# The fourth weight sum of the down projection: VectorE additions, or accumulating transfers within SBUF

## The chip, the cores and the metric

One NeuronCore of a Trainium2 chip. The metric is the device time of one execution in microseconds (us). The engines are named as the profile names them: PE (TensorE, matmul), DVE (VectorE), ACT (ScalarE), POOL (GpSimd) and SP (SyncE, which here only starts transfers). Transfers started by SP go through one queue, those started by POOL through another, and both are served by the same 16 DMA engines. A transfer that adds to its destination instead of overwriting it is started by POOL in this kernel.

## What is computed

One decoder layer on 512 positions of 2048 features: a mixer (a gated short convolution beside an mLSTM), a normalisation, a gated feed-forward part with a short convolution, and a second normalisation. The change lies in the last matrix product of the feed-forward part, the down projection.

```
hid = x @ w_up                         # 512 x 2048 times 2048 x 11264
hid = causal_dwconv(hid, w_ffn_conv, b_ffn_conv)
val, gate = hid[:, :5632], hid[:, 5632:]
ff  = (silu(gate) * val) @ w_down      # 512 x 5632 times 5632 x 2048
out = layer_norm(alpha * x + ff)
```

All inputs are float32. The kernel gets float32 accuracy from reduced-precision products: each operand is split into a high part and a low part (the operand less its high part), and three products of parts are added up (`mm3`).

## The kernel before

The down projection works by Strassen's scheme in Winograd's form: instead of eight block products there are seven, named P1, P2, P6, P5, P7, P3 and P4 in the order in which they run (`ORDER`, with index i from 0 to 6). Their operands are blocks of the weights and of the hidden activations, or sums of blocks. The weights have four blocks, A11, A12, A21 and A22, each 128 partitions by 1024 columns for every pair of contraction tiles. They are held in SBUF in the buffers `da11`, `da12`, `da21`, `da22`, and a fifth buffer `dx` takes a sum.

The contraction is cut into six chunks of 4, 4, 4, 4, 3 and 3 pairs (`CHUNK_PAIRS`; c is the chunk, p the pair). One chunk runs its seven products one after the other, each over all pairs. A slot is one (c, i, p): 12 matmuls. There are 154 slots.

Four weight sums are made for each pair:

- S1: `da21` += A22, an accumulating transfer from HBM, started by POOL, two pairs at a time (`down_s1`, L686);
- S2: `dx` = `da21` + `da11`, an addition on DVE (`down_s2`, L1669), the operand of P6;
- S3: `da11` += A21, an accumulating transfer from HBM (`down_s3`, L694), the operand of P7;
- S4: `da12` += `dx`, an addition on DVE (`down_s4`, L1681, its instruction at L1685), the operand of P3.

S4 may run when S2 of that pair is done and when P2, which uses `da12` as it was, has had its operand of that pair split. The next chunk's S2 overwrites `dx` and therefore waits for S4.

For each slot ACT makes the weights' high part (`down_split`, L1065) and DVE the low part (`down_lo_part`, L1651, recorded at L1655), into one of five slot buffers. Both work four slots ahead of PE (`DOWN_AHEAD`); a buffer comes free when PE has done the slot five before. The hidden activations of a product are split likewise, ACT's part in `hid_split` (L1086, recorded at L1101) and DVE's at L1663 or L1666.

PE's results stand in PSUM. DVE adds them to `acc` in SBUF (`add_out`, L1687, recorded at L1698), two halves a product, in the first two slots of the following product; a few products are the first for their part of `acc` and are copied by ACT (L1127). A product may start when the one two before has been taken out of PSUM.

DVE runs its work in one hand-written order: for each slot s the low part of slot s + 4, then `add_out`, then the weight sums that `sums_after(s)` (L361) names. S4 of pair 0 comes after the last slot of i = 1, of pairs 1 and 2 after that of i = 2, and of pair 3 after that of i = 3. S2 of the next chunk's pairs 0 and 1 comes after i = 5, pair 2 after i = 6.

POOL's order for a chunk (loop at L736): t1 and t2 (subtractions on hidden blocks; not in chunk 0, where DVE does them), S3 in two transfers, t3, t4 (subtractions again, L719 and L725), S1 of the next chunk in two transfers once `da21` has been loaded. In chunks 0 and 1 transfers that add the residual to `acc` (`add_residual`) stand in between. An instruction that waits holds up everything behind it on POOL.

SP's order for the next chunk is `load_hidden` and `load_block` in turn (L534, L529). The first of them waits for t4; the later ones wait until a buffer's operand has been split for the last time. In the up projection, which runs before, the fourth sum of that product is already made by such a transfer within SBUF: `up_s4`, recorded at L667, half a MB each.

Of the kernel before, what the change touches and what calls it, by code (L numbers as in the profile page):

```python
# [7 lines left out]
ALU = mybir.AluOpType  # L8
# [26 lines left out]
CHUNK_PAIRS = [4, 4, 4, 4, 3, 3]  # L35
# [95 lines left out]
def build(nc, x_t, x_rows, w_mix, w_out, w_up, w_down, b_gates, conv_w, gain, ln1_cols, ffn_conv,  # L131
          ln1_rows, ln2_rows, ident_in, head_rows_in, causal_in, out):
    ctx = ExitStack()
    with ctx:
        def at(name, shape, offset, dt=F32):
            return nc.alloc_sbuf_tensor_at(name, shape, dt, offset=offset)

        def sem(name):
            return ctx.enter_context(nc.semaphore(name))
# [75 lines left out]
        da12 = at("da12", [P, 4, 1024], XB + 16 * KB)  # L215
        da21 = at("da21", [P, 4, 1024], XB)
        da22 = at("da22", [P, 4, 1024], XB + 32 * KB)
        dx = at("dx", [P, 4, 1024], XB + 48 * KB)
# [74 lines left out]
        s2_down, s4_down = sem("s2_down"), sem("s4_down")  # L293
        t1_sum, t2_sum, t3_sum, t4_sum = sem("t1_sum"), sem("t2_sum"), sem("t3_sum"), sem("t4_sum")
        hc_lo = sem("hc_lo")
        down_hi, down_lo, down_done, half_done = sem("down_hi"), sem("down_lo"), sem("down_done"), sem("half_done")
# [36 lines left out]
        def unit_of(n):  # L333
            return n // NP + 1, n % NP
# [14 lines left out]
        def slot_no(c, i, p):  # L349
            return SLOT0[c] + i * CHUNK_PAIRS[c] + p  # L350
# [10 lines left out]
        def sums_after(s):  # L361

            c, i, p = DOWN[s]
            g = CHUNK_PAIRS[c]
            todo = []
            if i == 0 and c == 0:
                todo.append(("S2", 0, p))
            elif i == 0 and p == 3:
                todo.append(("S2", c, 3))
            if i in (1, 2, 3) and p == g - 1:  # L370
                todo += [("S4", c, a) for a in {1: [0], 2: [1, 2], 3: [3]}[i] if a < g]
            if i in (5, 6) and p == g - 1 and c + 1 < CHUNKS:
                todo += [("S2", c + 1, a) for a in {5: [0, 1], 6: [2]}[i]]
            return todo

        def out_blocks(c):
# [220 lines left out]
        def _(pool):  # L597
# [96 lines left out]
            def down_s3(c, p):  # L694

                n, w = sum(CHUNK_PAIRS[:c]) + p, min(2, CHUNK_PAIRS[c] - p)
                pool.wait_ge(s2_down, n + w)
                pool.wait_ge(down_lo, slot_no(c, 0, p) + w)
                pool.dma_start(da11[:, p:p + w, :], w_down[A21, :, 1024 * n:1024 * (n + w)].rearrange("p (k n) -> p k n", k=w),
                               accum_op=ALU.add, max_dma_last_dim=4096).then_inc(s3_added[p // 2], 16)  # L700

            def down_t1(c, g):
                for b in range(2):
                    pool.wait_ge(hb_in[b], 16 * (c + 1))
                pool.wait_ge(hc_lo, NP * c)
                pool.tensor_tensor(hy[:, 0:g, :], hb12[:, 0:g, :], hb11[:, 0:g, :], ALU.subtract).then_inc(t1_sum, 1)

            def down_t2(c, g):
                pool.wait_ge(hb_in[3], 16 * (c + 1))
                pool.wait_ge(t1_sum, OUT_CHUNKS + c + 1)  # L710
                pool.wait_ge(hc_lo, NP * c + 1)
                pool.tensor_tensor(hb11[:, 0:g, :], hb22[:, 0:g, :], hy[:, 0:g, :], ALU.subtract).then_inc(t2_sum, 1)

            def down_t3(c, g):
                pool.wait_ge(hb_in[3], 16 * (c + 1))
                pool.wait_ge(t1_sum, OUT_CHUNKS + c + 1)
                if c == 0:
                    pool.wait_ge(down_lo, slot_no(0, 3, 0))
                pool.tensor_tensor(hb12[:, 0:g, :], hb22[:, 0:g, :], hb12[:, 0:g, :], ALU.subtract).then_inc(t3_sum, 1)  # L719
# [16 lines left out]
            for c in range(CHUNKS):  # L736
                g = CHUNK_PAIRS[c]
                if c:
                    down_t1(c, g)
                    down_t2(c, g)  # L740
                for p in range(0, g, 2):
                    down_s3(c, p)
                down_t3(c, g)
                if c == 1:
                    add_residual(0, 1, NP)
                down_t4(c, g)
                if c == 0:
                    add_residual(0, 0, 2)
                if c + 1 < CHUNKS:
                    for p in range(0, CHUNK_PAIRS[c + 1], 2):  # L750
                        down_s1(c + 1, p)
                if c == 0:
                    add_residual(1, 1, 5)
                    add_residual(1, 0, 6)
            pool.wait_ge(out_bias, 16 * BIAS_BY_DMA)
            n = 0
# [8 lines left out]
        def _(act):  # L765
# [276 lines left out]
            for n in range(N_UP):  # L1042
                m, i = unit_of(n)
# [6 lines left out]
                if n in (3, 4):  # L1050
                    t, c = n - 3, 4 * (n - 3)
# [13 lines left out]
            def down_split(s):  # L1065

                c, i, p = DOWN[s]
                what = ORDER[i]
                if s < DOWN_SLOTS:
                    act.wait_ge(up_done, min(N_UP - 2 + s, N_UP))  # L1070
                else:
                    act.wait_ge(down_done, s - DOWN_SLOTS + 1)
                n = sum(CHUNK_PAIRS[:c]) + p
                if what in ("P1", "P2", "P4"):
                    if p == 0:
                        act.wait_ge(da_in[BLOCK[what]], 16 * (c + 1))
                elif what in ("P5", "P7"):
                    if p % 2 == 0:
                        act.wait_ge({"P5": s1_added, "P7": s3_added}[what][p // 2],
                                    16 * (OUT_CHUNKS + sum(CHUNK_PAIRS[a] > p for a in range(c + 1))))  # L1080
                else:
                    act.wait_ge({"P6": s2_down, "P3": s4_down}[what], n + 1)
                src = (da11, da12, da21, da22, dx)[BLOCK[what]]
                act.activation(dslot_hi[s % DOWN_SLOTS][:, :], src[:, p, :], ACT.Copy).then_inc(down_hi, 1)

# [27 lines left out]
            for s in range(N_DOWN):  # L1113
                c, i, p = DOWN[s]
# [30 lines left out]
        def _(dve):  # L1145
# [313 lines left out]
            for s in range(N_OUT):  # L1459
                k, p = s // OUT_PAIRS, s % OUT_PAIRS  # L1460
                c, i = k // NP, k % NP
# [161 lines left out]
            for n in range(N_UP):  # L1623
                m, i = unit_of(n)
# [44 lines left out]
            def down_s2(c, p):  # L1669

                if p == 0:
                    dve.wait_ge(da_in[A11], 16 * (c + 1))
                if p % 2 == 0:
                    dve.wait_ge(s1_added[p // 2], 16 * (OUT_CHUNKS + sum(CHUNK_PAIRS[a] > p for a in range(c + 1))))
                if c:
                    dve.wait_ge(s4_down, sum(CHUNK_PAIRS[:c]))
                else:
                    dve.wait_ge(up_done, N_UP - NP + 4)
                dve.tensor_tensor(dx[:, p, :], da21[:, p, :], da11[:, p, :], ALU.add).then_inc(s2_down, 1)  # L1679

            def down_s4(c, p):  # L1681
                n = sum(CHUNK_PAIRS[:c]) + p
                dve.wait_ge(s2_down, n + 1)
                dve.wait_ge(down_lo, slot_no(c, 1, p) + 1)
                dve.tensor_tensor(da12[:, p, :], da12[:, p, :], dx[:, p, :], ALU.add).then_inc(s4_down, 1)  # L1685

            def add_out(k, u):  # L1687

# [11 lines left out]
            def out_stats(row, fd):  # L1700
                for q in (2 * fd, 2 * fd + 1):
                    dve.bn_stats(bstat[:, row, q, :], acc[:, row, 512 * q:512 * q + 512]).then_inc(ln_step, 1)  # L1702
# [33 lines left out]
            for s in range(N_DOWN):  # L1736
                c, i, p = DOWN[s]
                k = NP * c + i
                if p == 0 and k < last_k:
                    hid_lo_part((k + 1) // NP, (k + 1) % NP)  # L1740
                if s + DOWN_AHEAD < N_DOWN:
                    down_lo_part(s + DOWN_AHEAD)
                if p < 2 and k and k - 1 not in FIRST_TOUCH:
                    add_out(k - 1, p)
                    th, fd = TARGET[ORDER[(k - 1) % NP]]
                    if c == CHUNKS - 1 and ORDER[i - 1] in ("P2", "P7", "P3") and i:
                        dve.wait_ge(added, 2 * (k - 1) + p + 1)
                        out_stats(2 * th + p, fd)
                if s == 0:
                    g = CHUNK_PAIRS[0]  # L1750
                    for b in range(2):
                        dve.wait_ge(hb_in[b], 16)
                    dve.tensor_tensor(hy[:, 0:g, :], hb12[:, 0:g, :], hb11[:, 0:g, :], ALU.subtract).then_inc(t1_sum, 1)
                if s == 1:
                    dve.wait_ge(hb_in[3], 16)
                    dve.wait_ge(t1_sum, OUT_CHUNKS + 1)
                    dve.wait_ge(hc_lo, 1)
                    dve.tensor_tensor(hb11[:, 0:g, :], hb22[:, 0:g, :], hy[:, 0:g, :], ALU.subtract).then_inc(t2_sum, 1)
                for what, chunk, pair in sums_after(s):
                    (down_s2 if what == "S2" else down_s4)(chunk, pair)  # L1760
            out_var(0, 12)
            out_var(1, 12)
            finish(0)
# [437 lines left out]
```

## Time and profile before

| | us |
|---|---|
| median of three runs | 2176.48 |
| lowest and highest run | 2165.42, 2182.86 |
| profiled execution, first to last instruction | 2176.2 |
| of it the down projection's matmuls, first to last start | 1724.94 to 2152.30 |
| mean granted TensorE clock, share of full | 0.994 |

The page gives for each engine its busy time in the span. The timeline lists instructions in order of start; the bracket at the end of a line is the time for which the engine had been idle, and what released it. Matmuls overlap, so their pace is read from the distance of their starts, not from the duration of one. The windows give the busy time of each engine in a stretch, the granted clock, and the mean busy share of the 16 DMA engines, which can come out a little above 1. Times are counted from the first instruction.

### The profile page before, as it was taken

How to read it: one execution, taken by the hardware profiler on the slowest of the kernel's cores; microseconds unless marked ns; L12 is line 12 of the kernel's file. 1: busy time of each engine (PE TensorE's matmuls, PEld its weight loads, DVE VectorE, ACT ScalarE, POOL GpSimd, SP SyncE). 2: the span in 40 equal slices, each digit the busy share in tenths (PEclk: the TensorE clock that was granted, in tenths of full speed). 3: DMA queues.
4: the chain of work that ended last, by engine and by line, in shares of the span. 5: the costliest groups of instructions: out<-in, count | busy, mean ns of one | idle time of the engine just before them, and what ended most of it. 6: DMA issues, size and time to landing. Idle time of an engine off the chain costs nothing. (4 is left out here: it accounts for less than half of the span.)

```text
span 2176.2 us, 26843 instructions
## 1 busy us (share of the span) xinstructions
PE 2125.9 (98%) x10583; PEld 1789.3 (82%) x10583; DVE 1594.2 (73%) x1860; ACT 948.3 (44%) x1107; POOL 267.1 (12%) x241
## 2 busy tenths in 40 slices
PE   9999999999999998999999999999999999999995
PEld 7888888888888887788888888888888788888874
DVE  4354324423338997988888888888888789999998
ACT  3332222221124446555555555555555464444442
POOL 0000000000001304011111111111111023221220
PEclk9999999999999999999999999999999999999998
DMA  6222222242227626888888887887778888775463
GB/s 238 97 97 78 92 89 91 78 171 98 98 79 232 181 73 162 219 241 231 218 207 210 238 219 197 212 229 209 187 203 209 274 228 219 210 237 145 140 193 78
DMA packets 93754, 375.88 MB, mean 173 GB/s; under 512 B 8908, under 2 KB 21228, under 8 KB 80320
## 3 DMA queue, kind: packets, MB, share of 16 engines
q1 hardware_dynamic: 63328, 263.22, 34.4%
q0 software_dynamic: 30304, 110.99, 26.3%
q8 instruction: 82, 1.34, 0.3%
q14 instruction: 40, 0.33, 0.0%
HBM read 326.46 MB, written 26.21 MB: 162 GB/s over the span
## 5 line engine op out<-in xcount | busy, mean ns | idle before, releaser
L1787 PE MATMUL ps<-xb,slot_hi 128*128 128x512 f32 x2408 | 854.5, 400 | 10.2 <-DVE hid L1532 9.8
L1788 PE MATMUL ps<-xb,slot_lo 128*128 128x256 f32 x2400 | 674.4, 281 | 0.0
L1787 PEld LDWEIGHTS ps<-xb,slot_hi 128*128 128x128 f32 x2408 | 453.8, 188 | 126.3 <-issue 12.5
L1788 PEld LDWEIGHTS ps<-xb,slot_lo 128*128 128x128 f32 x2400 | 454.1, 189 | 0.0
L772 ACT ACTIVATE w_hi<-raw 128x2048 fp32r<-128x2048 f32 x56 | 107.3, 1917 | 424.5 <-PE ps L1783 422.0
L1154 DVE TENSOR_TENSOR w_lo<-raw,w_hi 128x2048 fp32r<-128x2048 f32 x55 | 125.8, 2287 | 213.7 <-ACT w_hi L772 213.7
L1781 PE MATMUL ps<-act_hi,w_hi 128*128 128x512 f32 x640 | 249.7, 390 | 0.0
L1783 PE MATMUL ps<-act_hi,w_lo 128*128 128x512 f32 x640 | 249.1, 389 | 0.0
L1782 PE MATMUL ps<-act_lo,w_hi 128*128 128x512 f32 x640 | 249.1, 389 | 0.0
L1501 DVE TENSOR_TENSOR slot_lo<-unit_odd,slot_hi 128x1024 fp32r<-128x1024 f32 x153 | 187.0, 1222 | 36.6 <-ACT slot_hi L974 36.4
L974 ACT ACTIVATE slot_hi<-unit_odd 128x1024 fp32r<-128x1024 f32 x154 | 162.7, 1057 | 106.6 <-PE ps L1788 79.0
L1501 DVE TENSOR_TENSOR slot_lo<-unit_even,slot_hi 128x1024 fp32r<-128x1024 f32 x147 | 179.6, 1222 | 36.0 <-ACT slot_hi L974 35.9
L974 ACT ACTIVATE slot_hi<-unit_even 128x1024 fp32r<-128x1024 f32 x147 | 155.3, 1057 | 93.8 <-PE ps L1788 79.2
L1532 DVE TENSOR_TENSOR hid<-hid,ps 128x256 f32<-128x256 f32 x301 | 126.0, 419 | 42.8 <-ACT hid L1008 32.1
L1781 PE MATMUL ps<-slot_hi,hc 128*128 128x512 f32 x372 | 145.6, 391 | 5.3 <-DVE acc L1698 4.1
L1008 ACT ACTIVATE hid<-ps 128x256 f32<-128x256 f32 x172 | 65.7, 382 | 188.3 <-PE ps L1788 188.3
L1782 PE MATMUL ps<-slot_lo,hc 128*128 128x512 f32 x372 | 144.8, 389 | 0.0
L1783 PE MATMUL ps<-slot_hi,hc 128*128 128x512 f32 x372 | 144.8, 389 | 0.0
L1781 PEld LDWEIGHTS ps<-act_hi,w_hi 128*128 128x128 f32 x640 | 120.1, 188 | 27.0 <-issue 2.3
L1783 PEld LDWEIGHTS ps<-act_hi,w_lo 128*128 128x128 f32 x640 | 120.1, 188 | 24.9
L1782 PEld LDWEIGHTS ps<-act_lo,w_hi 128*128 128x128 f32 x640 | 120.2, 188 | 24.6
L1542 DVE SCALAR_TENSOR_TENSOR yy<-hid,fc,yy 128x511 f32<-128x511 f32 (+1 forms) x172 | 128.4, 747 | 3.9 <-ACT yy L1020 0.9
(238 smaller groups left out, 3431.8 us busy)
## 6 DMA issues: line engine op xcount, KB each, us to landing
raw<-w_mix SPq DMA_DIRECT2D x56, 1024.0 KB, 4.9
unit_odd<-w_up SPq DMA_DIRECT2D x88, 512.0 KB, 6.4
unit_even<-w_up SPq DMA_DIRECT2D x84, 512.0 KB, 6.5
da<-w_down SPq DMA_DIRECT2D x16, 2048.0 KB, 12.6
unit_odd<-w_up POOLq DMA_DIRECT2D x44, 512.0 KB, 8.8
unit_even<-w_up POOLq DMA_DIRECT2D x42, 512.0 KB, 8.4
da<-w_down POOLq DMA_DIRECT2D x20, 1024.0 KB, 9.8
oa<-w_out SPq DMA_DIRECT2D x6, 2048.0 KB, 8.1
```

Of the source, the lines that this page charges most:

```text
L772: act.activation(w_hi[:, s % SPLIT, :], raw[:, s % RAW, :], ACT.Copy).then_inc(tile_hi, 1)
L974: act.activation(slot_hi[(n + 2) % 3][:, :], unit[m % 2][:, BLOCK[ORDER[i]], :], ACT.Copy).then_inc(up_hi, 1)
L1008: act.activation(hid[g % 2][:, t, 256 * half:256 * half + 256], ps[:, up_bank(m, i), 0:256], ACT.Copy).then_inc(hid_act, 1)
L1154: dve.tensor_tensor(w_lo[:, s % SPLIT, :], raw[:, s % RAW, :], w_hi[:, s % SPLIT, :].bitcast(F32), ALU.subtract).then_inc(tile_lo, 1)
L1501: dve.tensor_tensor(lo_slot(n)[:, :], unit[m % 2][:, BLOCK[ORDER[i]], :], slot_hi[(n + 2) % 3][:, :].bitcast(F32), ALU.subtract).then_inc( ...
L1532: dve.tensor_tensor(x, x, cross, ALU.add).then_inc(hid_dve, 1)
L1542: dve.scalar_tensor_tensor(yy[:, t, lag:SEQ], hid[g % 2][:, t, 0:SEQ - lag], fc[:, c + 2 - lag:c + 3 - lag], yy[:, t, lag:SEQ], ALU.mult, ...
L1781: pe.matmul(dst, a[0], b[0], start=first, stop=False, skip_group_check=onto)
L1782: pe.matmul(dst, a[0], b[1], start=False, stop=False, skip_group_check=onto)
L1783: return pe.matmul(dst, a[1], b[0], start=False, stop=last, skip_group_check=onto)
L1787: pe.matmul(dst, a[0], b, start=first, stop=False, skip_group_check=onto)
L1788: return pe.matmul(dst[:, 256:512], a[1], b[:, 0:256], start=False, stop=last, skip_group_check=onto)
```

## The change

S4 is made by POOL's transfers. `down_s4` on DVE and its place in `sums_after` are gone. POOL gets a `down_s4` that starts a transfer from `dx` to `da12` that accumulates, for two pairs at a time (one for the last of a chunk of three): two a chunk, 1 MB for two pairs. It stands in POOL's order behind t3, and ahead of `add_residual` in chunk 1 and of t4. The semaphore `s4_down` now counts 16 a transfer. ACT's split of P3's first pair waits for both transfers of the chunk, where it waited pair by pair; DVE's S2 of the next chunk waits for the same two.

```diff
-            if i in (1, 2, 3) and p == g - 1:
-                todo += [("S4", c, a) for a in {1: [0], 2: [1, 2], 3: [3]}[i] if a < g]
...
+            def down_s4(c, p):
+
+                n, w = sum(CHUNK_PAIRS[:c]) + p, min(2, CHUNK_PAIRS[c] - p)
+                pool.wait_ge(s2_down, n + w)
+                pool.wait_ge(down_lo, slot_no(c, 1, p) + w)
+                pool.dma_start(da12[:, p:p + w, :], dx[:, p:p + w, :], accum_op=ALU.add).then_inc(s4_down, 16)
...
                 down_t3(c, g)
+                for p in range(0, g, 2):
+                    down_s4(c, p)
                 if c == 1:
                     add_residual(0, 1, NP)
                 down_t4(c, g)
...
-                else:
-                    act.wait_ge({"P6": s2_down, "P3": s4_down}[what], n + 1)
+                elif what == "P6":
+                    act.wait_ge(s2_down, n + 1)
+                elif p == 0:
+                    act.wait_ge(s4_down, 32 * (c + 1))
...
-                    dve.wait_ge(s4_down, sum(CHUNK_PAIRS[:c]))
+                    dve.wait_ge(s4_down, 32 * c)
...
-            def down_s4(c, p):
-                n = sum(CHUNK_PAIRS[:c]) + p
-                dve.wait_ge(s2_down, n + 1)
-                dve.wait_ge(down_lo, slot_no(c, 1, p) + 1)
-                dve.tensor_tensor(da12[:, p, :], da12[:, p, :], dx[:, p, :], ALU.add).then_inc(s4_down, 1)
...
-                for what, chunk, pair in sums_after(s):
-                    (down_s2 if what == "S2" else down_s4)(chunk, pair)
+                for chunk, pair in sums_after(s):
+                    down_s2(chunk, pair)
```

## Rows read from the trace of the kernel before

**Rows 1.** the page, part 1: busy us of each engine (share of the span) x instructions

```profile
PE 2125.9 (98%) x10583; PEld 1789.3 (82%) x10583; DVE 1594.2 (73%) x1860; ACT 948.3 (44%) x1107; POOL 267.1 (12%) x241
```

**Rows 2.** the timeline of PE: start us, us, engine, line, what [idle <-releaser]

```profile
1724.94 0.50 PE L1781 MATMUL ps<-slot_hi,hc 128*128 128x512 f32 x1 [0.46 <-DVE slot_lo L1655]
1804.19 0.39 PE L1781 MATMUL ps<-dslot_hi,hc 128*128 128x512 f32 x1
1815.07 0.39 PE L1781 MATMUL ps<-slot_hi,hc 128*128 128x512 f32 x1
1826.89 0.39 PE L1782 MATMUL ps<-slot_lo,hc 128*128 128x512 f32 x1
1935.49 0.39 PE L1781 MATMUL ps<-slot_hi,hc 128*128 128x512 f32 x1
2041.34 0.39 PE L1783 MATMUL ps<-dslot_hi,hc 128*128 128x512 f32 x1
2125.79 0.39 PE L1783 MATMUL ps<-dslot_hi,hc 128*128 128x512 f32 x1
2127.87 0.47 PE L1781 MATMUL ps<-slot_hi,hc 128*128 128x512 f32 x1 [1.70 <-DVE acc L1698]
2152.30 0.39 PE L1783 MATMUL ps<-dslot_hi,hc 128*128 128x512 f32 x1
```

**Rows 3.** the instructions of line 1685: ns min/median/max, first and last start, forms

```profile
L1685 DVE TENSOR_TENSOR da<-da,dx x22: 1208/1211/1219, 1752.5 to 2121.1; 128x1024 f32<-128x1024 f32 x22
```

**Rows 4.** the timeline of DVE near the end, columns as in Rows 2

```profile
2119.97 2.35 DVE L1685 TENSOR_TENSOR da<-da,dx 128x1024 f32<-128x1024 f32 x2
2124.24 1.21 DVE L1698 TENSOR_TENSOR acc<-acc,ps 128x1024 f32<-128x1024 f32 x1
2126.51 1.21 DVE L1698 TENSOR_TENSOR acc<-acc,ps 128x1024 f32<-128x1024 f32 x1
```

**Rows 5.** the timeline of POOL in chunks 0 and 2

```profile
1752.74 5.49 POOL L719 TENSOR_TENSOR hb<-hb,hb 128x1024 f32<-128x1024 f32 x1 [4.38 <-DVE slot_lo L1655]
1758.18 3.39 POOL L725 TENSOR_TENSOR hy<-hb,hb 128x1024 f32<-128x1024 f32 x1
1893.95 2.87 POOL L719 TENSOR_TENSOR hb<-hb,hb 128x1024 f32<-128x1024 f32 x1
```

**Rows 6.** the instructions of line 667, the up projection's own such transfer

```profile
L667 POOL DMA_DIRECT2D unit_odd<-unit_odd x22: 846/846/856, 861.5 to 1700.3; - x22
```

**Rows 7.** the windows: us, busy by engine, PEclk, DMA share, GB/s

```profile
1756.00:1760.00 4.00, 4.00 (x20) 3.29 (x18) 4.00 (x3) 1.10 (x2) 4.00 (x2) 1.00 0.00 0
1760.00:1764.00 4.00, 3.79 (x17) 2.89 (x16) 4.00 (x4) 3.33 (x4) 2.71 (x2) 1.00 0.27 82
1764.00:1768.00 4.00, 4.00 (x20) 3.30 (x19) 4.00 (x4) 2.64 (x3) 0.00 (x0) 1.00 1.03 200
1800.00:1804.00 4.00, 4.00 (x20) 3.30 (x19) 3.42 (x3) 1.08 (x2) 2.65 (x2) 1.00 1.06 231
```

**Rows 8.** the DMA queues, 1440 to 1500 us: packets, MB, share of 16 engines

```profile
q0 software_dynamic: 1296, 4.72, 40.5%
```

**Rows 9.** the timelines of DVE and ACT around the next chunk and in chunk 2

```profile
1793.03 2.35 DVE L1679 TENSOR_TENSOR dx<-da,da 128x1024 f32<-128x1024 f32 x2
1799.84 1.21 DVE L1698 TENSOR_TENSOR acc<-acc,ps 128x1024 f32<-128x1024 f32 x1
1810.99 1.22 DVE L1655 TENSOR_TENSOR slot_lo<-da,slot_hi 128x1024 fp32r<-128x1024 f32 x1
1927.27 1.21 DVE L1655 TENSOR_TENSOR slot_lo<-da,slot_hi 128x1024 fp32r<-128x1024 f32 x1
1772.77 1.04 ACT L1084 ACTIVATE slot_hi<-da 128x1024 fp32r<-128x1024 f32 x1
1808.76 1.06 ACT L1101 ACTIVATE hc<-hb 128x1024 fp32r<-128x1024 f32 x1 [6.02 <-DMA hb<-h_dram]
```

**Rows 10.** the DMA issues, 1777 to 1778.5 us: what, count, KB, us to landing

```profile
da<-w_down POOLq DMA_DIRECT2D x1, 1024.0 KB, 14.6
```

More of the change, by code:

```diff
@@ L366, in sums_after @@
             if i == 0 and c == 0:
-                todo.append(("S2", 0, p))
+                todo.append((0, p))
             elif i == 0 and p == 3:
-                todo.append(("S2", c, 3))
-            if i in (1, 2, 3) and p == g - 1:
-                todo += [("S4", c, a) for a in {1: [0], 2: [1, 2], 3: [3]}[i] if a < g]
+                todo.append((c, 3))
             if i in (5, 6) and p == g - 1 and c + 1 < CHUNKS:
-                todo += [("S2", c + 1, a) for a in {5: [0, 1], 6: [2]}[i]]
+                todo += [(c + 1, a) for a in {5: [0, 1], 6: [2]}[i]]
             return todo
```

## The prediction

> **What bounds the kernel now.** I read the page's first part first: PE is busy 98% of the span and DVE 73% [rows 1]. That average mixes stages, so the stretch of the change has to be read by itself, and the timeline of PE gives it. The down projection's 1848 matmuls (154 slots of 12) start between the first and the last row of [rows 2], at 1724.94 and 2152.30 us. Between the rows at 1826.89 and 2041.34 lie 946 steps without a wait, so a step is 214.45 / 946 = 0.2267 us and a slot 2.72 us. All 1847 steps at that pace would take 418.7 us; they take 427.4. So PE waits only 8.7 us in the whole stretch, and that is the most that relieving DVE there can return. It is 0.4% of the time.
>
> The timeline of DVE says which of these waits the removed additions make. The largest one stands at the end: PE's step at 2125.79 is followed at 2127.87, released by `add_out` [rows 2]. DVE had run two S4 additions from 2119.97, and the `add_out` rows that PE waited for stand behind them [rows 4]. The other waits either lie before chunk 0's first S4 addition (I assign those to the start of the stage) or follow a DVE operation drawn out beside a POOL subtraction; neither is S4's doing.
>
> **What the change removes.** 22 additions of 1.21 us [rows 3], two of them 2.35 us together [rows 4], so about 1.14 us each in a row: 25 us less on DVE. On the path that counts much less of it. In chunks 1 to 4 PE runs on at its pace through the S4 additions, so there PE's matmuls are the cover and the gain is zero. At the end the wait is 2.08 - 0.23 = 1.85 us, and the last `add_out` ends at 2126.51 + 1.21 = 2127.72. Without the two additions in front it ends some 2.3 us sooner, at 2125.4, before PE's last step of that product is through. I take the whole 1.85 us, and after it the order at the end of the kernel moves up with PE, since the final additions and normalisation follow PE's products. Bounds: 0 (the wait finds another cause) to 8.7 us (all waits go). I take 1.9, since only this wait has S4 directly in front.
>
> **What it adds on POOL.** Two DMA issues a chunk, 12 in all. The nearest row is the up projection's own accumulating transfer within SBUF, 0.85 us an issue [rows 6]. They come behind `down_t3` and ahead of `down_t4`. In chunk 2 t3 ends at 1893.95 + 2.87 = 1896.8, both conditions hold by then (P2's splits are done), and t4 waits for a later split anyway: cost zero. In chunk 0 t4 followed t3 at once, 1758.18 [rows 5], so t4, and the SP queue's `load_hidden(1, 0, ..)` that waits for it, go 1.7 us later; that load belongs to the next chunk, 46 us on, and costs nothing by itself. Work behind them on POOL (`add_residual`, `down_s1`) moves as much.
>
> **What it adds on the DMA engines.** In 1440 to 1500 us the POOL queue moved 4.72 MB in 40.5% of 60 us: 24.3 us of all 16 engines, 5.15 us a MB, within-SBUF transfers among them [rows 8]. A 1 MB transfer (1.05 in the unit of that row) is then 5.4 us, a pair 10.8 us. Lower bound for a pair: 0, if it only fills idle engines. Upper bound: twice that, 21.6 us, because the new transfers move 8 KB runs where the other accumulating ones move at most 4 KB a packet (4.72 MB / 1296 is 3.6 KB). I take 10.8: same queue, same operation.
>
> **Where the transfers must be in time.** P3's first split waits for both now. In chunk 2 the pair can go at 1896.8; P3's first low part was made at 1927.27 [rows 9], and PE takes that slot at 1935.49 [rows 2]. So 30 us are there before any engine waits, about 36 before PE does, against 10.8: zero. Chunks 1, 3, 4 and 5 have the same order. In chunk 0 t3 came late, because it waits for the low parts of P6: its row ends at 1752.74 + 5.49 = 1758.2 [rows 5]. P3's first split began at 1772.77 [rows 9]. From 1759 the pair has the engines to itself until some 1763.5 (share 0.00, then 0.27 [rows 7]), and shares them afterwards. It lands at about 1770 to 1774, and PE takes the slot only 8 slots before the one at 1804.19, at 1782.4. So zero again, with some 6 us to spare.
>
> **Where the gain can be lost.** From 1764 to 1804 the DMA engines are full: [rows 7] show the first and the last of ten stretches of 4 us, all at 0.97 or more. In that time chunk 1's blocks arrive. Of chunk 0's 10.8 us about 4 fit into the idle stretch before 1763.5, so 6.8 us of transfers are pushed ahead of, or between, those loads. Two of them have no slack left. S1 of chunk 1, issued at 1778, took 14.6 us [rows 10], to 1792.6, and DVE's S2 began at 1793.03 [rows 9]. And ACT waited 6.02 us for the hidden block that P2 of chunk 1 needs [rows 9]. How much of a delay reaches PE: behind S2 on DVE stands the `add_out` that ended at 1799.84 + 1.21 = 1801.1, which PE needs at 1804.19, so 3.1 us are free; behind the ACT wait stands the low part that ended at 1810.99 + 1.22 = 1812.2, which PE needs at 1815.07, so 2.9 are free. A delay of 6.8 us leaves 6.8 - 3.0 = 3.8 us of PE wait, once, since a wait at the first place makes room at the second. Bounds: 0 (the pushed work falls on the residual's transfer, which nobody waits for) to 21.6 - 4 - 3 = 14.6 us at the upper price. I take 3.8, as the POOL queue serves S4 ahead of S1. Chunk 2's first loads also follow a pair, but there the engines have free time; I set nothing.
>
> The sum: 2176.2 - 1.9 + 3.8 = 2178.1 us, against 2176.5 for the median of the runs shown, which stands 0.3 above the profiled span. The runs spread from 2165 to 2183, so about 1% (22 us) is what a measurement can tell from no change.
>
> The Trainium skill ("DMA: Bandwidth & Descriptors", section "Anatomy of one DMA — SWDGE (gpsimd) path") fits such a transfer as 2.0 us plus its bytes at 436 GB/s. The POOL queue's 5.15 us a MB [rows 8] speak for less than half that speed where the transfer accumulates. By the page a pair would hold the engines for an estimated 4.8 us, the pushed work would be under 1 us, and the sum would be rival A's.
>
> **The rivals.** *Forecast, 0.55:* a small gain and a small new wait at chunk 1, 2178 us, its own range 2174 to 2182.
>
> *A, 0.25: the transfers are hidden altogether.* The pair runs mostly in the idle stretch, or the delay falls on the residual. For it: 0.00 share at 1756 to 1760 [rows 7]. Against it: the ten full stretches after. It gives 2176.2 - 1.9 = 2174.3 us.
>
> *B, 0.13: 8 KB runs accumulate at half the speed.* For it: none of that length is in the trace. Against: the bytes and the engines are the same. The pair of chunk 0 then lands past 1780 and PE waits up to 14.6 us there; later chunks still have 30 us for 21.6. It gives 2176.2 - 1.9 + 14.6 = 2188.9 us.
>
> *C, 0.05: slower by more than 1%.* The place is P3's split in every chunk. It decides from 36 us a pair on, 3.3 times the price taken. At 43 us chunks 1 to 3 lose 7 each and chunk 0, which has about 20, loses 23: 2176.2 - 1.9 + 44 = 2218 us. Against it: no accumulating row is near that.
>
> *D, 0.02: faster by over 1%.* The 8.7 us of waits can't give 22.
>
> Faster by over 1%: 0.02; within 1%: 0.91 (forecast, A and nearly all of B); slower: 0.07. The range takes A, the forecast and B with the spread of the runs: 2167 to 2190 us.
>
> **What would show it.** No line for S4 on DVE, DVE some 25 us less busy; two POOL issues near 1758 and near 1897; PE's wait before the slot that stood at 2127.87 gone; PE waits near 1804 or 1815 of 0 to 5 us, with ACT's wait on the hidden block, or DVE's on S1, longer than before; landing of the new transfers at 6 to 14 us. The sum would be wrong if ACT waits for these transfers at P3, if PE's waits in chunk 1 exceed 6 us, or if PE's pace changes from 0.2267 us while they run.

## The result: 0.37% slower, and the profile after

| | before | changed |
|---|---|---|
| median, us | 2175.36 (22 runs) | 2181.43 (22 runs) |
| lowest and highest, us | 2163.56, 2182.86 | 2174.36, 2187.80 |
| ratio, 95% interval | | 1.0037 [1.0025, 1.0049] |
| profiled span, us | 2176.2 | 2181.9 |
| mean granted TensorE clock | 0.994 | 0.991 |

The kernel became slower by 0.37%, some 8 us (5.4 to 10.7 by the interval). The medians differ by 6.1 us, but that of the changed kernel falls into a gap: its runs form two bands, eleven from 2174 to 2180 and eleven from 2183 to 2188. Those of the kernel before spread as widely, from 2164 to 2183.

The page of the changed kernel, the engines' busy time:

```profile
PE 2122.7 (97%) x10583; PEld 1789.1 (82%) x10583; DVE 1570.3 (72%) x1838; ACT 948.2 (43%) x1107; POOL 275.7 (13%) x253
```

DVE is busy 23.9 us less than in [rows 1] (1594.2 - 1570.3), close to the 25 predicted, and the time still rose. Where it went is read from the starts of PE's slots. The table gives the time from the start of one slot to that of another, in us, the last column up to the start of the last matmul. Slots 28 to 55 are chunk 1, and slot 32 is the first of its P2.

| kernel | 0-4 | 4-28 | 28-36 | 36-144 | 144-last | ratio to before |
|---|---|---|---|---|---|---|
| before | 11.78 | 67.47 | 22.39 | 296.71 | 29.01 | |
| before, second trace | 14.37 | 67.50 | 25.00 | 296.77 | 28.97 | |
| changed | 13.94 | 68.25 | 32.69 | 296.85 | 27.02 | 1.0037 [1.0025, 1.0049] |
| changed, second trace | 14.69 | 67.07 | 34.41 | 296.78 | 27.05 | |
| e1: chunk 0 by DVE | 12.17 | 67.52 | 26.76 | 296.78 | 27.01 | 0.9994 [0.9977, 1.0012] |
| e2: only chunk 0 by transfers | 12.66 | 67.02 | 33.87 | 296.69 | 29.02 | 1.0046 [1.0028, 1.0064] |
| e3: changed, hidden block early | 12.06 | 67.33 | 23.48 | 296.89 | 27.05 | 0.9991 [0.9972, 1.0010] |
| e4: before, hidden block early | 11.24 | 67.52 | 21.76 | 296.62 | 29.00 | 0.9985 [0.9966, 1.0004] |
| e5: changed, hidden rows 4 KB | 11.02 | 66.95 | 21.95 | 296.89 | 27.03 | 0.9997 [0.9976, 1.0018] |
| e6: before, hidden rows 4 KB | 10.98 | 66.13 | 21.76 | 296.62 | 29.01 | 0.9989 [0.9972, 1.0007] |
| e7: S4 in runs of 4 KB | 11.02 | 66.51 | 34.49 | 296.84 | 27.01 | 1.0055 [1.0033, 1.0078] |
| e8: residual later | 11.50 | 67.02 | 29.58 | 296.85 | 27.06 | 1.0036 [1.0015, 1.0057] |
| e9: e3 and e5 together | 11.02 | 67.19 | 21.92 | 296.89 | 27.03 | 1.0002 [0.9984, 1.0020] |

One column gained: slots 144 to the last, 2.0 us. One lost: slots 28 to 36, 10.3 us. Between them, over 108 slots (the end of chunk 1, chunks 2 to 4 and half of chunk 5), all rows agree within 0.3 us, whoever makes S4.

The timeline of PE in the changed kernel, as in [rows 2]. The lines are the start of slot 28, the last matmul before slot 32, the first three of slot 32, then the last of slot 144 and the first of slot 145:

```profile
1801.45 0.39 PE L1784 MATMUL ps<-dslot_hi,hc 128*128 128x512 f32 x1
1812.11 0.39 PE L1786 MATMUL ps<-slot_hi,hc 128*128 128x512 f32 x1
1821.20 0.76 PE L1784 MATMUL ps<-slot_hi,hc 128*128 128x512 f32 x1 [8.71 <-ACT acc L1136]
1821.76 0.63 PE L1785 MATMUL ps<-slot_lo,hc 128*128 128x512 f32 x1
1822.19 0.63 PE L1786 MATMUL ps<-slot_hi,hc 128*128 128x512 f32 x1
2133.49 0.39 PE L1786 MATMUL ps<-dslot_hi,hc 128*128 128x512 f32 x1
2133.71 0.39 PE L1784 MATMUL ps<-slot_hi,hc 128*128 128x512 f32 x1
```

At 2133.71, the place that stood at 2127.87 in [rows 2], PE goes on in step, 0.22 us after the matmul before it; the wait of 1.85 us is gone. At slot 32 a new wait of 9.09 - 0.23 = 8.86 us stands, and the steps behind it are 0.43 us long where 0.2267 is the pace. It was released by ACT's copy of a finished product into `acc` (L1136, L1127 in the kernel before). ACT's timeline says why that copy was late (L1110 is the split of a hidden block, L1093 that of a weight block):

```profile
1816.29 1.06 ACT L1110 ACTIVATE hc<-hb 128x1024 fp32r<-128x1024 f32 x1 [16.29 <-DMA hb<-h_dram]
1817.25 1.04 ACT L1093 ACTIVATE slot_hi<-da 128x1024 fp32r<-128x1024 f32 x1
1818.19 1.00 ACT L1136 ACTIVATE acc<-ps 128x1024 f32<-128x1024 f32 x1
1819.10 1.04 ACT L1093 ACTIVATE dslot_hi<-da 128x1024 fp32r<-128x1024 f32 x1
1820.05 1.01 ACT L1136 ACTIVATE acc<-ps 128x1024 f32<-128x1024 f32 x1
```

ACT stood 16.29 us at the load of chunk 1's hidden block for P2, against 6.02 in [rows 9]. The copies of P4's two halves stand behind that split on ACT, and P2 may start only when both have left PSUM. Measured from the start of slot 28, ACT went on 14.84 us after it, and 4.57 in the kernel before: 10.27 later. The same two copies in the kernel before:

```profile
1810.67 1.00 ACT L1127 ACTIVATE acc<-ps 128x1024 f32<-128x1024 f32 x1
1812.52 1.02 ACT L1127 ACTIVATE acc<-ps 128x1024 f32<-128x1024 f32 x1
```

They ended at 1812.52 + 1.02 = 1813.54, PE took slot 32 at 1815.07 [rows 2], so 1.5 us were free. 10.27 - 1.5 = 8.8 is the new wait. The windows show what followed it (us, busy time of PE, PEld, DVE, ACT and POOL, then PEclk, DMA share, GB/s):

```profile
1820.00:1822.00 2.00, 0.80 (x2) 0.73 (x3) 1.23 (x1) 2.00 (x4) 0.00 (x0) 0.50 0.94 338
1822.00:1824.00 2.00, 2.00 (x6) 1.52 (x6) 1.96 (x2) 2.00 (x4) 0.00 (x0) 0.50 0.09 27
```

After the wait PE ran at 0.50 of full clock, the lower of its two levels (1.2 GHz). The eight steps from 1821.20 to 1824.67 took 3.47 us instead of 1.81, 1.7 us more. The wait, the slow steps and a wait at slot 36 that was 0.2 shorter make 8.86 + 1.66 - 0.23 = 10.3, the column's difference.

The first column also rose by 2.2 us in the first pair of traces. It lies before any S4, and the second trace of the kernel before shows 14.37 there, so the kernel before has it too. Nor are the 5.7 us by which this execution reached the down projection sooner (slot 0 at 1719.26, and 1724.94 in [rows 2]).

### The profile page after: what moved, and what is told of

It is laid out like the page before. It is cut to its first block and busy times, and to the rows that moved or that the text cites. A ratio compares the mean times of both kernels' runs of the same rounds, so it can differ in the third digit from the quotient of the medians.

```text
span 2181.9 us, 26807 instructions
## 1 busy us (share of the span) xinstructions
PE 2122.7 (97%) x10583; PEld 1789.1 (82%) x10583; DVE 1570.3 (72%) x1838; ACT 948.2 (43%) x1107; POOL 275.7 (13%) x253
```

## Experiments: which transfer costs it

Theory 1 says that chunk 0's pair of transfers pushes back the loads of chunk 1's hidden block. Rival 2 says that each transfer costs something in every chunk, and rival 3 that the wait at the start of the stage belongs to the change. Two kernels split the change by chunk.

**e1_chunk0_dve.** Chunk 0's four sums on DVE again, the others by transfers:

```diff
-                for p in range(0, g, 2):
-                    down_s4(c, p)
+                if c:
+                    for p in range(0, g, 2):
+                        down_s4(c, p)
...
+                dve.tensor_tensor(da12[:, p, :], da12[:, p, :], dx[:, p, :], ALU.add).then_inc(s4_out, 1)
```

> The changed kernel, with chunk 0's four S4 sums made by DVE as before and chunks 1 to 5 by transfers. Theory 1 (the loss is chunk 0's pair of transfers, which pushes back the loads of chunk 1's hidden block on the full DMA engines): PE's wait of 9 us before slot 32 is gone, the gain at the end stays, so about 2 us under the kernel before, 2173 us, and some 8 to 10 under the changed kernel. Rival 2 (each transfer within SBUF costs PE, DVE or POOL something in every chunk): five of six parts of the loss stay, 2180 us. Rival 3 (the wait at the start of the stage, 3.15 us and the clock after it, is the change's doing): it would stay, about 2177 us.

Measured: 2176.28 us, ratio 0.9994 [0.9977, 1.0012]. The loss is gone, although ten of the twelve transfers are left; the time is 3 us above the 2173 expected, and does not by itself tell theory 1 from rival 3's 2177. The gain at the end is there (27.01). Its own trace has 26.76 in slots 28 to 36, because ACT still waited 10.41 us, and PE 3.0 before slot 32:

```profile
1813.26 1.06 ACT L1115 ACTIVATE hc<-hb 128x1024 fp32r<-128x1024 f32 x1 [10.41 <-DMA hb<-h_dram]
```

That is between the kernels, and led to the second traces below.

**e2_only_chunk0.** The kernel before, with only chunk 0's sums by transfers:

```diff
-            if i in (1, 2, 3) and p == g - 1:
+            if c and i in (1, 2, 3) and p == g - 1:
...
+                if c == 0:
+                    for p in range(0, g, 2):
+                        pool_s4(c, p)
```

> The kernel before, with only chunk 0's S4 sums made by two transfers within SBUF and chunks 1 to 5 by DVE. Theory 1: the whole loss and none of the gain at the end: ACT waits 16 us for chunk 1's hidden block, PE 9 us before slot 32, 10 us over the kernel before, 2185 us. Rival 2: a sixth of the loss, 2177 us. Rival 3: 2179 us.

Measured: 2187.39 us, ratio 1.0046 [1.0028, 1.0064], the whole loss from two transfers. ACT's wait for the hidden block, and PE's:

```profile
1818.46 1.06 ACT L1113 ACTIVATE hc<-hb 128x1024 fp32r<-128x1024 f32 x1 [17.49 <-DMA hb<-h_dram]
...
1823.37 0.77 PE L1793 MATMUL ps<-slot_hi,hc 128*128 128x512 f32 x1 [9.91 <-ACT acc L1139]
```

The end column is 29.02, as in the kernel before: no gain where the last chunk's sums stay on DVE. Rival 2 asked for 2177 us here and 2180 in e1, and falls in both. Rival 3 asked for 2179 here; the first column is 12.66, inside what the kernel before shows by itself.

**e10_before_again and e11_after_again.** Both kernels once more, for a second trace.

> The kernel before once more, for a second trace of it: how much the landing of chunk 1's hidden block, and with it the time of slots 28 to 36, varies by itself. If the wait of ACT varies by several us (6.0 in the first trace), the wait of 10.4 us in the changed kernel with chunk 0's sums on DVE is such a variation; if it comes out at 6 again, that kernel has a delay of its own that is not explained.

> The changed kernel once more, for a second trace of it: slots 28 to 36 take 32 to 35 us again, with ACT's wait at 15 us or more; the wait at slot 4 (3.15 us in the first trace, before any S4) comes out near the 1 us of the kernel before, if it is no part of the change.

Measured, first the kernel before:

```profile
1809.94 1.06 ACT L1101 ACTIVATE hc<-hb 128x1024 fp32r<-128x1024 f32 x1 [8.63 <-DMA hb<-h_dram]
```

and the changed kernel:

```profile
1818.95 1.06 ACT L1110 ACTIVATE hc<-hb 128x1024 fp32r<-128x1024 f32 x1 [17.41 <-DMA hb<-h_dram]
```

The kernel before varies from 6.0 to 8.6 us of waiting, and its slots 28 to 36 from 22.4 to 25.0; the changed kernel from 16.3 to 17.4, and from 32.7 to 34.4. The two don't meet: by which trace is set against which, the change adds 7.7 to 11.4 us to the wait. The 10.4 of e1 lies nearer the kernel before, but above both its traces; what made up the rest is open. The wait at slot 4 did not come out near 1 us, as expected if it is no part of the change, but at 3.7; in the kernel before it was 3.3 this time, so it varies in both.

## Experiments: why the load is late

**e3_hidden_early and e4_before_hidden_early.** SP issues the block's load behind `da21` of the next chunk, instead of behind `da12`; the same edit in the changed kernel and in the kernel before:

```diff
                 load_block(c + 1, A21, da21)
+                load_hidden(c + 1, 2, hb21)
                 sp.wait_ge(hc_lo, NP * c + 5)
...
-                sp.wait_ge(hc_lo, NP * c + 7)
-                load_hidden(c + 1, 2, hb21)
```

> The changed kernel, with the load of the next chunk's hidden block for P2 (buffer hb21) issued by SP right behind the block da21 instead of behind da12, so that it is ahead of 4 MB of weights on SP's queue; its buffer is free after t4. Theory 1: ACT's wait of 16.3 us before slot 32 falls to 0 to 5 us and PE's wait there to under 1 us: some 10 us under the changed kernel, 2171 us, unless S1, now behind that load, makes DVE wait (then up to 3 us more). Rival 2: no change against the changed kernel, 2181 us.

> The kernel before, with the same earlier load of the hidden block. Theory 1: PE did not wait at slot 32 there, ACT's 6.0 us lay inside its lead: within 1 us of the kernel before, 2175 us, so that the load's place is worth something only together with the transfers. Rival: the load's place is worth the same 10 us in both kernels, 2165 us.

Measured: 2175.57 us, ratio 0.9991 [0.9972, 1.0010], for the changed kernel, and 2175.24, 0.9985 [0.9966, 1.0004], for the kernel before. In the first of them ACT no longer waits for a transfer:

```profile
1803.40 1.06 ACT L1109 ACTIVATE hc<-hb 128x1024 fp32r<-128x1024 f32 x1 [1.71 <-PE ps L1785]
```

Slots 28 to 36 fall from 32.69 to 23.48, with S4's transfers all in place; in the kernel before from 22.39 to 21.76. So the whole loss passes through this one load, and its place is worth 9 to 11 us in that column with the transfers and 0.6 to 3.2 without them. With this wait gone, DVE waited 3.2 us for S1, the other place that the prediction had named; PE's lead covered all but 0.3 us of it, before slot 28. The 1.7 us by which the column stands over that of e4 are mostly a wait at slot 36, behind an `add_out`. The time came out 4.6 us above the 2171 expected.

The remaining question is what delays it by 10 us, when the pair holds the engines for that long in all and part of that is idle time. The delay starts at SP's first load for chunk 1, `load_hidden(1, 0, ..)`. From issue to landing, the last number of a line, it took in the kernel before and in the changed kernel:

```profile
hb<-h_dram SPq DMA_DIRECT2D x1, 512.0 KB, 4.8
hb<-h_dram SPq DMA_DIRECT2D x1, 512.0 KB, 15.9
```

It took 4.9 us in e1 and 15.9 in e2: it is late where chunk 0's pair goes by transfers. Issued at 1757.76, it meets the pair, which landed at 1762.8 and 1767.5. Behind it on SP's queue stands `da21`, for which S1 waits. Later on that queue come the weight block `da12` and the late hidden block, in the kernel before:

```profile
da<-w_down SPq DMA_DIRECT2D x1, 2048.0 KB, 21.1
hb<-h_dram SPq DMA_DIRECT2D x1, 512.0 KB, 23.6
```

and in the changed kernel:

```profile
da<-w_down SPq DMA_DIRECT2D x1, 2048.0 KB, 25.4
hb<-h_dram SPq DMA_DIRECT2D x1, 512.0 KB, 33.9
```

They were issued equally long before slot 28 in both kernels (21.9 and 19.2 us). From its issue `da12` took 4.3 us more, the hidden block 10.3 (8.8 in the second traces, 26.2 and 35.0). The DMA queues of the changed kernel while SP's hidden blocks were under way (packets, MB, share of 16 engines; q0 is POOL's, q1 SP's), from 1784 to 1788 us:

```profile
q0 software_dynamic: 169, 0.69, 87.3%
q1 hardware_dynamic: 165, 0.17, 15.5%
```

and from 1808 to 1812:

```profile
q0 software_dynamic: 189, 0.72, 89.6%
q1 hardware_dynamic: 188, 0.19, 17.3%
```

The two queues move packet for packet, 169 to 165 and 189 to 188. POOL's packets carry 4 KB, SP's 1 KB, since a row of a hidden block is 256 columns; so SP gets 0.17 to 0.19 MB in 4 us, under 50 GB/s, as long as POOL's queue has work. The Trainium skill ("DMA: Bandwidth & Descriptors", section "Queues, rings and completion order") says that a DMA engine takes turns between its queues a packet at a time; the trace agrees, 189 to 188.

**e5_hidden_4k and e6_before_hidden_4k.** The hidden activations are stored so that a load reads 4 KB in a row for a chunk of four tiles; again in both kernels:

```diff
-        h_dram = nc.dram_tensor("h_dram", (NF, P, SEQ), F32).ap()
+        h_dram = nc.dram_tensor("h_dram", (2, P, NF, 256), F32).ap()
...
-                             h_dram[t:t + pairs, :, 256 * (b % 2):256 * (b % 2) + 256].rearrange("k p t -> p k t")
+                             h_dram[b % 2, :, t:t + pairs, :]
```

> The changed kernel, with the hidden activations stored so that a block's load reads 4 KB in a row for each partition instead of rows of 1 KB. Theory 1a (the load of the hidden block is late because its 1 KB packets go one for one with the POOL queue's packets of 4 to 8 KB): ACT's wait of 16.3 us before slot 32 falls under 6, PE's wait there is gone, about 10 us under the changed kernel, 2171 us; the wait at the start of the stage shrinks as well. Theory 1b (it is late because of the volume of the pair alone, 10.8 us of all engines): the load still lands some 10 us later than in the kernel before with the same rows, PE waits 5 us or more, 2178 us or over.

> The kernel before, with the same longer rows of the hidden activations. Control for the run of the changed kernel with them. Theory 1a: PE did not wait for these loads there, so within 2 us of the kernel before, 2174 to 2177 us, and the changed kernel with long rows is then about 2 us under this one, by the gain at the end. Theory 1b: this one is 5 us or more under the changed kernel with long rows.

Measured: 2174.07 us, ratio 0.9997 [0.9976, 1.0018], for the changed kernel, and 2175.20, 0.9989 [0.9972, 1.0007], for the kernel before. The changed kernel came out 3 us above the 2171 expected and 1.1 under its control, where 2 were expected; none of these differences is clear of the intervals. In it SP's queue now gets a larger part, here again from 1784 to 1788 us:

```profile
q0 software_dynamic: 117, 0.48, 60.7%
q1 hardware_dynamic: 109, 0.60, 39.3%
```

0.60 MB, where it had 0.17. ACT's wait for the block is 3.46 us, and PE does not wait for it (21.95 in slots 28 to 36):

```profile
1802.77 1.06 ACT L1111 ACTIVATE hc<-hb 128x1024 fp32r<-128x1024 f32 x1 [3.46 <-DMA hb<-h_dram]
```

In the kernel before with the same rows the block is there before ACT asks:

```profile
1804.14 1.06 ACT L1102 ACTIVATE hc<-hb 128x1024 fp32r<-128x1024 f32 x1 [1.70 <-PE ps L1784]
```

With the pair in place and longer rows the column is the same as without the pair. But most of the delay remains. From issue to landing the block took, with long rows, in the kernel before and in the changed one:

```profile
hb<-h_dram SPq DMA_DIRECT2D x1, 512.0 KB, 13.9
hb<-h_dram SPq DMA_DIRECT2D x1, 512.0 KB, 21.1
```

That is 7.2 us more with the pair, where the short rows had 8.8 to 10.3 more. So the landing comes out nearer theory 1b, PE's wait as theory 1a has it: the block lands 9.7 us sooner to begin with (13.9 against 23.6), and the delay falls inside PE's lead. What the pair still costs here shows before slot 28, the first place that the prediction had named:

```profile
1802.11 0.47 PE L1785 MATMUL ps<-dslot_hi,hc 128*128 128x512 f32 x1 [1.18 <-DVE acc L1702]
```

DVE had waited 4.2 us for S1 there, and not at all in e6; the column from 4 to 28 is 0.8 us longer than e6's.

**e7_s4_4k.** S4's transfers cut to runs of 4 KB:

```diff
-                pool.dma_start(da12[:, p:p + w, :], dx[:, p:p + w, :], accum_op=ALU.add).then_inc(s4_down, 16)
+                pool.dma_start(da12[:, p:p + w, :], dx[:, p:p + w, :], accum_op=ALU.add,
+                               max_dma_last_dim=4096).then_inc(s4_down, 16)
```

> The changed kernel, with S4's transfers cut to runs of 4 KB instead of 8 KB. If a packet's length sets how long a 1 KB packet of the hidden load waits for its turn, S4's own part of the delay halves at the most, and PE's wait of 9 us falls by 2 to 4: 2178 us. If the volume counts, no change: 2181 us, with the landing of S4 the same (7 to 15 us) and issues of 1.2 us instead of 0.85.

Measured: 2187.13 us, ratio 1.0055 [1.0033, 1.0078]; slots 28 to 36 took 34.49. The issues became longer, the landing did not become shorter:

```profile
L705 POOL DMA_DIRECT2D da<-dx x12: 886/1677/2188, 1750.1 to 2105.5; - x12
DMA to landing us min/median/max: 8.0/10.6/17.9
```

The time lies above both expected ones, and its interval overlaps that of the changed kernel. The length of S4's own runs is not what costs: the first load of chunk 1 still took 16.3 us to land. S4 itself had landed 12 us before the late block was issued; what that block meets on POOL's queue is the residual and S3.

**e8_residual_later.** Chunk 0's first residual transfer behind S1 instead of ahead of it:

```diff
-                if c == 0:
-                    add_residual(0, 0, 2)
                 if c + 1 < CHUNKS:
...
                 if c == 0:
+                    add_residual(0, 0, 2)
                     add_residual(1, 1, 5)
```

> The changed kernel, with chunk 0's first residual transfer (1 MB, accumulating, on the POOL queue) issued behind S1 of chunk 1 instead of ahead of it. Theory 1 (POOL's queue is what holds the loads back): some 5 us of POOL's transfers leave the stretch before S1, S1 is issued earlier, PE's wait before slot 32 falls by 3 to 6 us, 2176 us. Rival (the delay is set by SP's own 4 MB of weights ahead of the block): no change, 2181 us.

Measured: 2182.86 us, ratio 1.0036 [1.0015, 1.0057]. In time this can't be told from the changed kernel. In the trace the wait is shorter, 13.20 us, and the column 29.58:

```profile
1815.28 1.06 ACT L1109 ACTIVATE hc<-hb 128x1024 fp32r<-128x1024 f32 x1 [13.20 <-DMA hb<-h_dram]
```

S1 was issued 25.9 us before slot 28, where it was 22.6 in the changed kernel, and 3.1 to 4.8 us of the column came back, at the low end of what theory 1 expected. The first load of chunk 1 landed 11.3 us after its issue instead of 15.9, and PE's wait before slot 32 was 5.8 us. POOL's work ahead of the load counts, though moving one transfer doesn't cure it. Theory 1's time of 2176 us was missed.

**e9_both.** The edits of e3 and e5 in one kernel.

> The changed kernel with both: the hidden block for P2 loaded earlier and the rows of 4 KB. If the load's lateness is the whole of the loss, nothing is left to win beyond the 4 KB rows alone: the slots 28 to 36 take 21.8 us, the end stays 2 us shorter than in the kernel before, 2173 us, 1 to 4 us under the kernel before. If the two act on different waits, 2170 us or less.

Measured: 2175.74 us, ratio 1.0002 [0.9984, 1.0020]. Slots 28 to 36 took 21.92, the same as with the long rows alone: both edits cure the same wait. The time was 2.7 us above the 2173 expected. None of these kernels is shown to beat the kernel before; the 2.0 us at the end are less than the interval.

## Why the prediction came out as it did

**The range and the sign of the sum held; the size did not.** The sum was +1.9 us, about 8 were measured, inside the 2167 to 2190. The columns give the same: 10.3 us lost less 2.0 gained is 8.3. That the time lies in the range is in part luck: the room above was there for rival B, which did not come, and the prediction's own sign of a wrong sum, waits of PE over 6 us in chunk 1, did (8.86 us).

**The gain at the end: right.** 1.9 us predicted for the wait behind the last chunk's S4 additions; 2.0 measured in every trace in which the last chunk's S4 is off DVE (27.01 to 27.06 against 28.97 to 29.02). Chunks 1 to 4 gave nothing, as predicted: slots 36 to 144 take 296.6 to 296.9 in all kernels.

**POOL's issues: right.** Those of chunk 0, with t3 ahead, t4 behind, and then S1's:

```profile
1749.23 4.36 POOL L724 TENSOR_TENSOR hb<-hb,hb 128x1024 f32<-128x1024 f32 x1 [4.38 <-DVE slot_lo L1664]
1753.53 1.77 POOL L705 DMA_DIRECT2D da<-dx  x2
1754.70 3.03 POOL L730 TENSOR_TENSOR hy<-hb,hb 128x1024 f32<-128x1024 f32 x1
1778.89 2.42 POOL L689 DMA_DIRECT2D da<-w_down  x2 [19.97 <-DMA da<-w_down]
```

The pair goes out as soon as t3 ends, and t4 starts 1.1 us after t3's end, where 1.7 was predicted. S1 is issued at 1778.89, 22.6 us before slot 28, where it was 26.2 before (1778.0 and 1804.19). That is 3.6 us less lead, and DVE waited only 0.71 us for it: the first of the two places named for the loss was not the one here, as it was in e5.

**The transfers: right, and rival B falls.** POOL's queue from 1756 to 1760 us, while it moved S4:

```profile
q0 software_dynamic: 96, 0.79, 101.4%
```

0.79 MB in 96 packets is 8.2 KB each, at 197 GB/s: 8 KB runs accumulate at the speed of the 4 KB ones, 5.3 us for 1.05 MB, where 5.4 was taken. The Trainium skill ("DMA: Bandwidth & Descriptors", section "Anatomy of one DMA — SWDGE (gpsimd) path") has 436 GB/s in its fit; the measurement decides, and says under half of that for this accumulating transfer. Landing:

```profile
L705 POOL DMA_DIRECT2D da<-dx x12: 846/1147/1714, 1753.5 to 2108.3; - x12
DMA to landing us min/median/max: 7.0/10.0/15.2
```

15.2 us at the longest, and no wait of ACT for these transfers: rival C's condition of 36 us was never near. Rival A, no new wait, falls with the one at slot 32.

**The step that failed: the delay at chunk 1, 3.8 us in the sum, 10.3 in the first trace and 9.4 in the second pair.** The place was right: chunk 1's hidden block for P2, at PE's slot 32. Four parts of it were wrong. First, SP's `load_hidden(1, 0, ..)` was said to cost nothing by itself; it took 15.9 us to land instead of 4.8, and chunk 1's other loads stand behind it. Second, the delay was reckoned as volume, 10.8 us less some 4 that fit into idle time, so 6.8; 10.27 were measured. With the long rows of e5 and e6 it was 7.2, near the 6.8, so 2 to 3 us go with the 1 KB rows, by one or two traces of each kernel. How the rest splits between waiting in SP's queue and sharing the engines is not shown. Third, 3.0 us were taken as free, by the low part that PE needs; the copies of P4 on ACT, behind the same split, left 1.5. The prediction looked at what stands behind the late instruction on DVE, and not on its own engine. Fourth, 1.7 us went to the lower clock after the wait, which the sum did not have.

What is not settled: the two bands of times, some 8 us apart, and the variation of slots 0 to 4 (11.0 to 14.7), which both kernels share. The bands are not the wait at slot 32 coming and going: the trace of e7 is of a run in its lower band (2180.89 us), and has the whole of it (34.49).

## What to carry to other kernels

Work taken off an engine that the critical engine doesn't wait for buys only the few waits in which it stands directly in front: here 25 us of DVE bought 2. A transfer put in its place is paid where the DMA engines are full, here some 60 us later and on another queue: look at every load that is issued while the transfer moves, even one that nobody needs soon, since others stand behind it; then for the next load whose waiter has little lead, and for what stands behind that waiter on its own engine. Loads in short rows moved slowly here while another queue was busy with long packets; lengthening their rows, or issuing the late one earlier, took PE's wait at slot 32 away.

## What the runs showed of the hardware

The two DMA queues took turns packet by packet, 189 to 188 with 4 KB packets against 1 KB and 117 to 109 with the long rows, so that 1 KB packets beside 4 KB accumulating ones moved at under 50 GB/s. An accumulating transfer within SBUF moved 197 GB/s with runs of 8 KB, and cutting them to 4 KB did not make it land sooner (10.0 and 10.6 us in the median). After a wait of 8.9 us PE came back at the lower clock (0.50), and kept it for some eight matmuls. The length of the wait alone does not decide: after 2.9 us at slot 4 of the same execution the clock was 0.50 too (1736 to 1738 us), after 3.0 us at slot 32 of e1 it was 1.00 (1818.2 to 1820.2 us).
